# A retention layer inside a one-core model kernel: value projections first, then the heads one after another through values, gate, transposes and output product

## What is computed

```python
proj = xn @ w_in                                  # xn: rmsnorm(h), 256 x 1024; w_in: 1024 x 6144
q, k, v, g = jnp.split(proj, [1024, 2048, 4096], axis=-1)
q = rotary(q.reshape(B, S, 4, 256), positions)    # 4 heads
k = rotary(k.reshape(B, S, 4, 256), positions) * 256 ** -0.5
v = v.reshape(B, S, 4, 512)
o = chunkwise_retention(q, k, v)                  # per head: (q k^T * decay) v
o = rmsnorm(o, gn_gain).astype(xn.dtype)          # per head, over its 512 values
return (jax.nn.silu(g) * o.reshape(B, S, 2048)) @ w_o   # w_o: 2048 x 1024
```

## Time and profile before

| | |
|---|---|
| median of three runs | 2779.85 us |
| the profiled execution: its own time / its span | 2772.44 us / 2770.6 us |
| granted TensorE clock, mean | 0.959 of full speed |
| TensorE matmul busy | 2581.4 us (93%) |
| VectorE busy | 1884.8 us (68%) |
| ScalarE busy | 1462.0 us (53%) |
| HBM read | 594.4 MB, 215 GB/s over the span |
| retention layer, from TensorE's first product of q to the end of its output product | 22.5 to 238.6 us of the span |

### The profile page before, as it was taken

The page is one execution under the profiler, slowest core; times in us unless marked ns, Lnnn a source line. Parts: engine busy times, 40 slices in busy tenths (PEclk is TensorE's granted clock), DMA queues, the critical chain, the costliest instruction groups (busy, mean ns, idle before and its releaser), DMA issues.

```text
span 2770.6 us, 32703 instructions
## 1 busy us (share of the span) xinstructions
PE 2581.4 (93%) x13559; PEld 2168.4 (78%) x13559; DVE 1884.8 (68%) x1960; ACT 1462.0 (53%) x1343; POOL 0.2 (0%) x4
## 2 busy tenths in 40 slices
PE   7989998996999999999999898899889999997999
PEld 7868897855887888888787776688668988875898
DVE  7455556435888888888888687658656565766555
ACT  3433334442776676767666565455544344555442
POOL 0000000000000000000000000000000000000000
PEclk9999999957999999999999999999989999998999
DMA  7535754415999999989999885255225545522554
GB/s 232 171 104 167 209 185 150 163 34 197 352 351 343 323 371 325 370 324 368 328 351 342 315 312 189 84 170 161 73 91 163 187 154 162 167 77 77 166 185 135
DMA packets 301811, 597.59 MB, mean 216 GB/s; under 512 B 13552, under 2 KB 105952, under 8 KB 301664
## 3 DMA queue, kind: packets, MB, share of 16 engines
q1 hardware_dynamic: 301664, 595.50, 62.4%
HBM read 594.41 MB, written 1.05 MB: 215 GB/s over the span
## 4 chain that ended last, share of the span: by engine, by line
PE 81%; DVE 12%; ACT 4%; issue 2%; DMA 1%; SPq 0%; DVEq 0%; ACTq 0%
PE ps L211 79%; DVE ring_rounded L705 3%; ACT high_rounded L692 1%; DVE arena_rounded L1874 1%; PE ps L1622 1%; PE ps L1210 1%; DMA ring<-in_w_down_dense 1%; DVE arena L2332 0%; DVE h L855 0%; DVE arena L2462 0%; DVE arena L2484 0%; DVE ring_rounded L1874 0%; DVE arena L2482 0%; DVE xT L642 0%; DVE xT_rounded L648 0%
## 5 line engine op out<-in xcount | busy, mean ns | idle before, releaser
L211 PE MATMUL ps<-high_rounded,arena_rounded 128*128 128x512 f32 x2664 | 834.7, 395 | 25.4 <-DVE arena_rounded L715 13.4
L705 DVE TENSOR_TENSOR ring_rounded<-ring,high_rounded 128x2048 fp32r<-128x2048 f32 (+3 forms) x231 | 513.4, 2230 | 320.0 <-ACT high_rounded L692 319.0
L692 ACT ACTIVATE high_rounded<-ring 128x2048 fp32r<-128x2048 f32 (+3 forms) x231 | 430.2, 1864 | 398.1 <-PE ps L211 383.7
L211 PEld LDWEIGHTS ps<-high_rounded,arena_rounded 128*128 128x128 f32 x2664 | 499.1, 190 | 131.5 <-DVE arena_rounded L715 16.4
L211 PE MATMUL ps<-ring_rounded,arena_rounded 128*128 128x512 f32 x1000 | 395.0, 395 | 0.0
L211 PE MATMUL ps<-xT_high_rounded,high_rounded 128*128 128x256 f32 x1280 | 363.7, 284 | 26.0 <-DVE xT_rounded L648 12.5
L211 PE MATMUL ps<-xT_high_rounded,ring_rounded 128*128 128x256 f32 x1280 | 361.8, 283 | 0.0
L211 PE MATMUL ps<-xT_rounded,high_rounded 128*128 128x256 f32 x1280 | 361.5, 282 | 0.0
L211 PE MATMUL ps<-arena_rounded 128*128 128x512 f32 x864 | 339.2, 393 | 0.0
L1874 DVE TENSOR_TENSOR arena_rounded<-arena,high_rounded 128x2048 fp32r<-128x2048 f32 x131 | 297.4, 2288 | 27.5 <-ACT high_rounded L1677 27.1
L1677 ACT ACTIVATE high_rounded<-arena 128x2048 fp32r<-128x2048 f32 x131 | 251.0, 1919 | 84.6 <-PE ps L211 83.2
(11 more groups left out here) (281 smaller groups left out, 3145.2 us busy)
## 6 DMA issues: line engine op xcount, KB each, us to landing
arena<-in_w_down_moe SPq DMA_DIRECT2D x76, 1024.0 KB, 5.3
arena<-in_w_up_moe SPq DMA_DIRECT2D x72, 1024.0 KB, 5.9
arena<-in_w_gate_moe SPq DMA_DIRECT2D x68, 1024.0 KB, 5.4
ring<-in_w_in SPq DMA_DIRECT2D x50, 1024.0 KB, 5.0
ring<-in_w_gate_moe SPq DMA_DIRECT2D x44, 1024.0 KB, 5.4
ring<-in_w_up_moe SPq DMA_DIRECT2D x40, 1024.0 KB, 5.8
ring<-in_w_down_moe SPq DMA_DIRECT2D x36, 1024.0 KB, 5.2
ring<-in_w_up SPq DMA_DIRECT2D x32, 1024.0 KB, 5.4
```

What stands on the lines that cost most here:

```text
L211: return self.pe.matmul(out, lhsT, rhs, start=start, stop=stop, skip_group_check=True)
L692: act.activation(as_rounded(m, m.highs[n % HIGHS][:, 0:size]), m.slots[n % RING][:, 0:size], ACT.Copy).then_inc(m.rounded, 1)
L705: dve.tensor_tensor(as_rounded(m, slot), slot, as_rounded(m, m.highs[n % HIGHS][:, 0:size]), ALU.subtract).then_inc(m.slabs_split, 1)
```

## The change

Four things move; no product, no weight and no activation function is added or dropped.

- **Order of the stages.** v (4 wide blocks), then q and k (8 tall slabs), then two gate blocks, the scores, the third gate block, and the fourth gate block by token tile between the first head's values and its transposes. The slabs are loaded in the new order.
- **The opening.** With `opening=True`, ScalarE rounds slab 0 ahead of the first token tile's parts and slab 1 between the tiles, and VectorE takes the remainders of both slabs between the tiles. TensorE starts v on the first token tile alone (`tensor_wide_first`). The tables for the rotary embedding are made after slab 3's remainder, and waited for only before q.
- **The heads.** Values, gated product, transposes, gain and rounding are done per head; one head's output product (two slabs) is spread around the next head's values and transposes. The mean, square root and reciprocal of both token tiles are done in one instruction each. The semaphore `gated` is gone.
- **The rounding calls** stand between these steps, one slab at a time.

```diff
@@ -270,10 +270,10 @@
 
     win = w["w_in_a"][0]
     out = []
+    for h in range(HEADS_R):
+        out += wide("r.v", win, 2048 + h * DV_R)
     for h in range(2 * HEADS_R):
         out += tall("r.qk", win, h * DK_R)
-    for h in range(HEADS_R):
-        out += wide("r.v", win, 2048 + h * DV_R)
     for h in range(HEADS_R):
         out += wide("r.g", win, 4096 + h * DV_R)
...
         L.up(m.n.drained, 4)
     for t in range(TT if casts else 0):
+        if opening:
+
+            scalar_split(act, L, m, 1 if t else -1)
         for half in range(2):
...
                                   ALU.subtract).then_inc(m.parted, L.up(m.parted))
+        if opening and t == 0:
+            vector_lows(dve, L, m, 0)
     if not keep:
...
+def tensor_head_values(pe, L, m, h):
+    v = lambda j: m.r_v[:, j, h * DV_R:(h + 1) * DV_R]
+    for t in range(TT):
+        pe.wait_ge(m.v.drained, L.room(m.v))
+        bank = L.bank(m.v)
+        if t == 0:
+            L.mm(bank, m.r_s[:, h, 0:P], v(0)).then_inc(m.v.full, L.up(m.v.full))
+        else:
+            L.give_back(L.mm(bank, m.r_s[:, h, P:S], v(0), True, False))
+            L.mm(bank, m.r_s[:, h, S:S + P], v(1), False, True).then_inc(m.v.full, L.up(m.v.full))
+
+
+def tensor_head_turned(pe, L, m, h):
+
+    pe.wait_ge(m.v.drained, L.emptied(m.v))
+    for t in range(TT):
+        bank = L.bank(m.v)
+        for c in range(4):
+            k = 4 * h + c
+            ins = pe.transpose(bank[:, c * P:(c + 1) * P], m.r_g[:, t, k * P:(k + 1) * P], m.ident)
+            if c == 3:
+                ins.then_inc(m.v.full, L.up(m.v.full))
+            else:
+                L.give_back(ins)
+
+
+def tensor_head_out(pe, L, m, h, half):
+    if half == 0:
+        pe.wait_ge(m.parted, L.next(m.parted))
+    if h == 0 and half == 0:
+        pe.wait_ge(m.acc_drained, L.sums_taken())
+    tensor_rows(pe, L, m, "r.out", parts(m, m.r_yT, m.r_yT_high), 4 * h + 2 * half, h == 0 and half == 0,
+                h == HEADS_R - 1 and half == 1)
+
+
 def tensor_retention(pe, L, m):
-    pe.wait_ge(m.parted, L.next(m.parted, 4))
+    x = parts(m, m.xT, m.xT_high)
+    tensor_wide_first(pe, L, m, "r.v", x, m.a)
+    for g in range(3):
+        tensor_wide(pe, L, m, "r.v", x, m.a)
     for h in range(2 * HEADS_R):
-        tensor_tall(pe, L, m, "r.qk", parts(m, m.xT, m.xT_high), m.v)
-    for g in range(4):
-        tensor_wide(pe, L, m, "r.v", parts(m, m.xT, m.xT_high), m.a)
+        tensor_tall(pe, L, m, "r.qk", x, m.v)
+    for g in range(2):
+        tensor_wide(pe, L, m, "r.g", x, m.a)
...
-    for g in range(4):
-        tensor_wide(pe, L, m, "r.g", parts(m, m.xT, m.xT_high), m.a)
+    tensor_wide(pe, L, m, "r.g", x, m.a)
     pe.wait_ge(m.v.drained, L.emptied(m.v))
     pe.wait_ge(m.a.drained, L.emptied(m.a))
+    tensor_head_values(pe, L, m, 0)
+    w = [L.slab("r.g"), L.slab("r.g")]
+    tensor_wide_tile(pe, L, m, w, 0, x, m.a)
+    tensor_head_turned(pe, L, m, 0)
+    tensor_wide_tile(pe, L, m, w, 1, x, m.a)
     for h in range(HEADS_R):
+        if h + 1 < HEADS_R:
+            tensor_head_values(pe, L, m, h + 1)
+        tensor_head_out(pe, L, m, h, 0)
+        if h + 1 < HEADS_R:
+            tensor_head_turned(pe, L, m, h + 1)
+        tensor_head_out(pe, L, m, h, 1)
...
+    def head_sums(h):
         for t in range(TT):
-            pe.wait_ge(m.v.drained, L.room(m.v))
-            bank = L.bank(m.v)
-            v = lambda j: m.r_v[:, j, h * DV_R:(h + 1) * DV_R]
-            if t == 0:
-                L.mm(bank, m.r_s[:, h, 0:P], v(0)).then_inc(m.v.full, L.up(m.v.full))
-            else:
-                L.mm(bank, m.r_s[:, h, P:S], v(0), True, False)
-                L.mm(bank, m.r_s[:, h, S:S + P], v(1), False, True).then_inc(m.v.full, L.up(m.v.full))
-    for t in range(TT):
-        if t == 0:
-            L.up(m.gated, 8)
-            pe.wait_ge(m.gated, L.at(m.gated))
-        for g in range(4):
-            pe.wait_ge(m.v.drained, L.room(m.v))
-            bank = L.bank(m.v)
-            for c in range(4):
-                k = 4 * g + c
-                ins = pe.transpose(bank[:, c * P:(c + 1) * P], m.r_g[:, t, k * P:(k + 1) * P], m.ident)
-                if c == 3:
-                    ins.then_inc(m.v.full, L.up(m.v.full))
-                else:
-                    L.give_back(ins)
-    tensor_out(pe, L, m, "r.out", parts(m, m.r_yT, m.r_yT_high), 0, 16, True)
-
-
-def scalar_retention(act, L, m):
-    scalar_split(act, L, m, 2 * HEADS_R)
+            act.wait_ge(m.v.full, L.next(m.v.full))
+            bank = m.ps[:, m.v.banks[(L.count[m.v.full] - 1) % 2], :]
+            act.activation(m.junk[:, t, 0:512], bank, ACT.Square, accum_out=m.small[:, t:t + 1]).then_inc(
+                m.sums, L.up(m.sums))
+        scalar_root(act, L, m, TT)
+        L.up(m.v.full, TT)
+
     for g in range(4):
         scalar_split(act, L, m, 2)
         for t in range(TT):
             act.wait_ge(m.a.full, L.next(m.a.full))
             bank = L.filled(m.a)
             act.activation(m.r_v[:, t, g * 512:(g + 1) * 512], bank, ACT.Copy).then_inc(m.a.drained, L.up(m.a.drained))
-    for g in range(4):
+        if g == 1:
+            scalar_constants(act, L, m)
+    scalar_split(act, L, m, 2 * HEADS_R)
+    for g in range(3):
         scalar_split(act, L, m, 2)
         for t in range(TT):
-            act.wait_ge(m.a.full, L.next(m.a.full))
-            bank = L.filled(m.a)
-            act.activation(m.r_g[:, t, g * 512:(g + 1) * 512], bank, ACT.Silu).then_inc(m.a.drained, L.up(m.a.drained))
-
+            gate(g, t)
     L.up(m.v.full, 1 + 2 * HEADS_R + HEADS_R)
-    for h in range(HEADS_R):
-        for t in range(TT):
-            n = 2 * h + t
-            act.wait_ge(m.v.full, L.next(m.v.full))
-            bank = m.ps[:, m.v.banks[(L.count[m.v.full] - 1) % 2], :]
-            act.activation(m.junk[:, n % 2, 0:512], bank, ACT.Square, accum_out=m.small[:, 0:1]).then_inc(
-                m.sums, L.up(m.sums))
-            scalar_root(act, L, m, 1)
-    scalar_split(act, L, m, 8)
+    head_sums(0)
+    scalar_split(act, L, m)
+    gate(3, 0)
+    scalar_split(act, L, m)
+    gate(3, 1)
+    for h in range(1, HEADS_R):
+        head_sums(h)
+        scalar_split(act, L, m, 2)
+    scalar_split(act, L, m, 2)
+
+
+def vector_head_gated(dve, L, m, h):
+
+    dve.wait_ge(m.sums, L.next(m.sums, TT))
+    rstd = vector_root(dve, L, m, TT, DV_R)
+    for t in range(TT):
+        dve.wait_ge(m.v.full, L.next(m.v.full))
+        bank = L.filled(m.v)
+        g = m.r_g[:, t, h * DV_R:(h + 1) * DV_R]
+        dve.scalar_tensor_tensor(g, bank, rstd[:, t:t + 1], g, ALU.mult, ALU.mult).then_inc(
+            m.v.drained, L.up(m.v.drained))
+
+
+def vector_head_turned(dve, L, m, h):
+    at = slice(4 * h, 4 * h + 4)
+    gain = m.gain[:, G_RET + 4 * h:G_RET + 4 * h + 4].unsqueeze(2).broadcast_to([P, 4, P])
+    for t in range(TT):
+        dve.wait_ge(m.v.full, L.next(m.v.full))
+        bank = L.filled(m.v).rearrange("p (c n) -> p c n", c=4)
+        dve.tensor_tensor(m.r_yT[:, at, t * P:(t + 1) * P], bank, gain, ALU.mult).then_inc(
+            m.v.drained, L.up(m.v.drained))
+    dve.wait_ge(m.v.drained, L.at(m.v.drained))
+    vector_split(dve, L, m, m.r_yT[:, at, :], m.r_yT_high[:, at, :])
 
 
 def vector_retention(dve, L, m):
 
+    for g in range(4):
+        vector_lows(dve, L, m, 2)
+        if g == 0:
+            vector_constants(dve, L, m)
+    dve.wait_ge(m.sines, L.next(m.sines, 2))
...
-    for g in range(4):
+    for g in range(2):
         vector_lows(dve, L, m, 2)
     dve.wait_ge(m.decay_in, L.next(m.decay_in, 16))
     for h in range(HEADS_R):
@@ -1028,31 +1098,18 @@
         bank = L.filled(m.v)
         dve.tensor_tensor(m.r_s[:, h, :], bank[:, 0:384], m.r_decay[:, h, :], ALU.mult).then_inc(
             m.v.drained, L.up(m.v.drained))
-    for g in range(4):
-        vector_lows(dve, L, m, 2)
-    L.up(m.a.drained, 16)
+    vector_lows(dve, L, m, 2)
+    L.up(m.a.drained, 14)
     dve.wait_ge(m.a.drained, L.at(m.a.drained))
     for h in range(HEADS_R):
-        for t in range(TT):
-            dve.wait_ge(m.v.full, L.next(m.v.full))
-            bank = L.filled(m.v)
-            dve.wait_ge(m.sums, L.next(m.sums))
-            rstd = vector_root(dve, L, m, 1, DV_R)
-            g = m.r_g[:, t, h * DV_R:(h + 1) * DV_R]
-            dve.scalar_tensor_tensor(g, bank, rstd, g, ALU.mult, ALU.mult).then_inc(m.v.drained, L.up(m.v.drained))
-
-    dve.wait_ge(m.v.drained, L.at(m.v.drained))
-    dve.memset(m.small[:, 189:190], 0.0).then_inc(m.gated, L.up(m.gated, 8))
-    for t in range(TT):
-        for g in range(4):
-            dve.wait_ge(m.v.full, L.next(m.v.full))
-            bank = L.filled(m.v).rearrange("p (c n) -> p c n", c=4)
-            gain = m.gain[:, G_RET + 4 * g:G_RET + 4 * g + 4].unsqueeze(2).broadcast_to([P, 4, P])
-            dve.tensor_tensor(m.r_yT[:, 4 * g:4 * g + 4, t * P:(t + 1) * P], bank, gain, ALU.mult).then_inc(
```

(35 more changed lines are left out.)

## The result

The changed kernel's median is 2756.6 us over 4 runs (2753.0 to 2759.3), that of the kernel before 2779.3 over 4 (2774.0 to 2782.1). The ratio is 0.9916, with a 95% interval of 0.9902 to 0.9929: faster by 22.7 us, where 16.7 was forecast (2763 us, range 2753 to 2774).

A forecast was written before the change was run, and what follows sets the result against it. TensorE's own work was taken to bound the kernel (81% of the span), with gains where it waits or runs at low clock. 1.7 + 1.6 + 7.2 + 4.3 + 1.9 = 16.7 us off 2779.85 gave 2763 us, range 2753 to 2774.

The forecast's parts named there:

- The sign it named for the layer: The retention layer's last output product was to come at 221 to 223 us instead of 238.6.
- Opening: Start of the layer: TensorE begins v on the first token tile at 20.8 us, 1.7 us sooner.
- Tables: Rotary tables behind slab 3's remainder: the 1.95 us wait goes, a new 0.3 us wait comes; 1.6 us gained.
- Values and transposes: Values and transposes done per head: 7.2 us gained in the values, 4.3 us in the transposes.
- Output product: The layer's output product: 1.9 us gained if TensorE's clock stays up between heads.
- Scores, q and k, gates: These stages hold the same products in another order: gain 0, with VectorE's slack as cover.
- The shift reaches the end whole: After the layer: loads start when a slab has been read, so what follows should shift by the full gain.
- ScalarE's order: Rival in the heads: slabs queue between squares and gates, 8 us lost; gain 8.7, 2771 us; chance 0.12.
- The time was not given back: Rival behind the layer: expert-weight loads bind and an earlier start waits for them; 2779 us, chance 0.08.
- The clock did not fall in the heads: Rival in the heads: TensorE's clock drops, 4.75 us per low output slab, up to 2801 us; chance 0.06.

The follow-up runs named there:

- second profile of before: The unchanged kernel before, run and profiled once more: median 2779.4 us, ratio 1.0007; its first layer's output product ended at 236.8 us.
- the late rounding: The changed kernel with slabs 0 and 1 rounded behind all parts of the activations, as before the change: 2758.3 us, ratio 0.9935 to the kernel before.
- the second comparison: Both kernels unchanged, run once more: the changed kernel's median 2756.6 us, ratio 0.9924 to the kernel before.
- one copy more: The changed kernel with one added 128x512 copy on ScalarE ahead of each head's square root: 2754.4 us (one run).
- five: The changed kernel with five added 128x512 copies on ScalarE ahead of each head's square root: 2762.9 us, ratio 0.9945 to the kernel before.
- the heads alone: The kernel before, in its old order and with its old opening, with only the per-head part of the change: 2760.5 us, ratio 0.9932.

## Why the prediction was right, step by step

The mechanism held at each place; its sum was 4.2 us short of the layer's gain in the first pair of profiles, 2.4 short of that against the second profile of before (19.1), and 6.0 short of the 22.7 between the medians, which lies within the range all the same. The sign it named for the layer, an end at 221 to 223 us, was passed by 3.3 us (217.7); the others came true, the start at 20.56, no wait over 0.5 us before the first values, none ahead of a group of transposes. That the first pair's spans differ by 16.4, near the 16.7 forecast, is chance: 4.4 us were lost again in later layers, where the changed code has no part.

- **Opening, 1.7.** Measured 1.95 (22.51 to 20.56), and 1.6 between the second profiles. The chain ran as worked out: rounding 14.46 to 16.37, parts, remainder to 20.42, where 20.8 was worked out. TensorE stood still for 4.8 us ahead of it (15.76 to 20.56), not for the 3.9 put there. Shown by the late rounding, worth 2.0. The clock was low at the start as expected (0.62 in 20.5 to 24.5), at a cost like that before: the first 48 products took 12.6 us where 48 x 0.2287 = 11.0 is full clock. That cost is not the same in each execution, 12.6 to 14.0 us in the profiles of the new order.
- **Tables, 1.6.** Read from the waits, 1.8: the 1.95 us are gone, and the new wait of 0.3 us for ScalarE's copy came to 0.12. The fit that was worked out at 0.1 us was 0.4. Against the second profile of before, where the tables cost 1.30, it is 1.2. No run took this part by itself.
- **Values and transposes, 7.2 + 4.3 = 11.5.** This is the term that was mis-sized. A head's period in after is 14.4 us (157.15 to 171.57 to 185.94), so values and transposes cost 14.4 - 11.0 = 3.4 us a head, where 2.84 + 1.42 was put. The rows' durations hold the tail of the last product, in which the next one already runs: eight transposes of 1.03 are followed after 0.79. And the 1.42 for eight came from a stretch in which the clock was falling; in the second profile of before they took 1.10 to 1.26. With 3.4, four heads and the 0.73 cost 14.3 instead of 29.3 us: 15.0 gained (13.7 against the second profile of before, in which the clock did not fall in the first transposes).
- **Output product, 1.9.** Clock at 1.00 in all of it. In before it took 45.8 us in the first profile and 45.7 in the second (191.12 to 236.84), each time with the clock low at its start.
- **Scores, q and k, gates, 0.** Some 0.3 us sooner, of which no part was looked into.
- **The shift reaches the end whole.** The medians bear it out, 22.7 and 21.5 us for 18.8 to 20.9 in the layer; a single pair of profiles can't show it, since the rest of the program scatters by 12 us between executions.

**The rivals.** ScalarE's order did not bind: slacks of 1.46, 1.42, 2.5 and 2.4 where 1.7, 1.6 and 2.8 were worked out; one copy more was free, five were not. The time was not given back: the second comparison has 21.5 us in the medians. The clock did not fall in the heads: it was at 1.00 with eight transposes at a time between at least 5.5 us of products, and it fell where TensorE had stood still for 3.9 us. The Trainium skill (TensorE: Matmul & The Clock Gate, section "Part 4: PE-mode transpose") says that a transpose does not count as activity of the engine as a product does, which spoke for that rival; in these traces groups of eight did no harm. Where before has 24 almost in a row, behind waits, the clock was at 0.63 in one profile and at 1.00 in the other, so what many of them do alone stays open.

## What to carry to other kernels

A chain over three engines that is done for several heads one after another costs its full length each time; put the next head's products, or any independent block, between a head's values and its transposes, and only a chain longer than that block is seen. Cost a small group of matmuls by the distance to the next one's start in a busy stream, not by the duration of its row, and take it from a stretch at the clock that will hold. Where a whole execution scatters by more than the effect, compare the end of the stage that was changed in each profile, and profile the kernel before twice.

## What was not expected

In two of the twelve profiles (the heads alone; first slabs rounded late) the 256-column products of the q and k stage came every 0.118 us, in the other ten every 0.113, at a granted clock of 1.00 and with no wait. The rows count 88 and 91 products that touch 10 us of it (the late rounding, then after):

```profile
85.00:95.00 10.00, 10.00 (x88) 10.00 (x87) 8.16 (x10) 3.84 (x2) 0.00 (x0) 1.00 0.59 186
```

```profile
85.00:95.00 10.00, 10.00 (x91) 10.00 (x90) 8.03 (x9) 2.99 (x2) 0.00 (x0) 1.00 0.59 195
```

It costs 1.7 us in the layer (from the first product to the first values 130.2 us instead of 128.4). Later in the program both spacings occur in every profile, after included. One place where the same kernel has the one in its first profile and the other in its second, at the same clock, is this (before, then before once more):

```profile
1815.00:1825.00 10.00, 10.00 (x87) 10.00 (x86) 4.50 (x7) 5.92 (x7) 0.00 (x0) 1.00 0.47 156
```

```profile
1815.00:1825.00 10.00, 10.00 (x91) 10.00 (x90) 6.40 (x12) 8.63 (x8) 0.00 (x0) 1.00 0.55 169
```

So at that place it goes with the execution and not with the build, and taking its 1.7 us out of the two runs above is fair as far as this shows. Those two were not profiled a second time, and the cause of the spacing stays open.
